# Five column sums of a hybrid trunk kernel: eight one-column products each, or four tiles of 32 columns, an ACT copy and a turn through DRAM

## The reference

```python
c_act = jax.nn.silu(c)
for i in range(DEPTH):
    mod = c_act @ ada_w[i] + ada_b[i]                       # (1, 6144)
    sh1, sc1, g1, sh2, sc2, g2 = jnp.split(mod[:, None, :], 6, axis=-1)
    h = rms_norm(x, norm_mix[i]) * (1.0 + sc1) + sh1
    y = mixer_i(h)                                          # attention or HGRN2
    x = x + g1 * y
    h = rms_norm(x, norm_ffn[i]) * (1.0 + sc2) + sh2
    x = x + g2 * swiglu(h, ffn_w1[i], ffn_w3[i], ffn_w2[i])
```

## Time and profile before

| | |
|---|---|
| time, median of 3 runs | 870.5 us (870.15 to 871.99) |
| profiled execution: its time, its span | 872.44 us, 870.6 us |
| mean granted PE clock | 0.99 |
| busy: PE, PEld, DVE | 839.7 us (96%), 699.8 us (80%), 613.9 us (71%) |
| busy: ACT, POOL | 432.6 us (50%), 137.9 us (16%) |
| DMA | 188.97 MB, mean 217 GB/s |

### The profile page before, as it was taken

The page is one execution under the profiler, slowest core; times in us unless marked ns, Lnnn a source line. Parts: engine busy times, 40 slices in busy tenths (PEclk is TensorE's granted clock), DMA queues, the critical chain, the costliest instruction groups (busy, mean ns, idle before and its releaser), DMA issues.

```text
span 870.6 us, 10955 instructions
## 1 busy us (share of the span) xinstructions
PE 839.7 (96%) x4254; PEld 699.8 (80%) x4254; DVE 613.9 (71%) x728; ACT 432.6 (50%) x549; POOL 137.9 (16%) x157
## 2 busy tenths in 40 slices
PE   4999999999999989999999989999999999999998
PEld 2778878878878878887888877888888788887886
DVE  4897798788888776577576676787867665654544
ACT  5355464464445555453344356778575744433431
POOL 3000101111010120011010020467813000000000
PEclk9799999999999999999999999999999999999999
DMA  9997878887877635688787745434234577665521
GB/s 320 365 357 238 293 253 276 283 255 234 284 260 235 229 108 193 198 275 293 260 271 255 240 145 180 156 98 146 97 117 129 208 248 234 228 206 180 192 96 49
DMA packets 122102, 188.97 MB, mean 217 GB/s; under 512 B 5683, under 2 KB 91048, under 8 KB 122052
## 3 DMA queue, kind: packets, MB, share of 16 engines
q1 hardware_dynamic: 109796, 146.10, 51.8%
q0 software_dynamic: 12256, 42.18, 14.4%
HBM read 187.18 MB, written 1.09 MB: 216 GB/s over the span
## 4 chain that ended last, share of the span: by engine, by line
PE 76%; DVE 13%; ACT 4%; issue 4%; DMA 2%; POOL 1%; SPq 0%; DVEq 0%; ACTq 0%; POOLq 0%
PE bank L526 62%; DVE wlo L1363 2%; PE bank L642 2%; DVE acc L1374 2%; DVE x L1532 2%; PE bank L722 2%; PE bank L748 1%; PE bank L916 1%; ACT whi L988 1%; PE bank L595 1%; PE bank L703 1%; PE bank L860 1%; DMA x<-in_x_dram 1%; PE bank L559 1%; DVE sq L1530 1%
## 5 line engine op out<-in xcount | busy, mean ns | idle before, releaser
L1363 DVE TENSOR_TENSOR wlo<-raw,whi 128x2048 fp32r<-128x2048 f32 x123 | 285.4, 2325 | 41.9 <-ACT whi L988 41.8
L988 ACT ACTIVATE whi<-raw 128x2048 fp32r<-128x2048 f32 (+1 forms) x124 | 235.3, 1900 | 18.9 <-DMA raw<-in_attn_w_qkv_dram 12.2
L526 PE MATMUL bank<-whi,hT_hi 128*128 128x512 f32 (+1 forms) x728 | 195.1, 391 | 2.4 <-ACT hT_hi L988 1.5
L526 PE MATMUL bank<-wlo,hT_hi 128*128 128x512 f32 (+1 forms) x752 | 194.1, 381 | 1.2 <-DVE wlo L1363 1.2
L526 PE MATMUL bank<-whi,hT_lo 128*128 128x512 f32 (+1 forms) x728 | 187.3, 380 | 0.0
L526 PEld LDWEIGHTS bank<-wlo,hT_hi 128*128 128x128 f32 x752 | 137.3, 188 | 29.5 <-DVE wlo L1363 2.0
L526 PEld LDWEIGHTS bank<-whi,hT_lo 128*128 128x128 f32 x728 | 132.9, 188 | 26.5
L526 PEld LDWEIGHTS bank<-whi,hT_hi 128*128 128x128 f32 x728 | 129.5, 188 | 29.9 <-issue 6.5
L393 POOL DMA_DIRECT2D ada_w<-in_ada_w_dram x80 | 42.7, 534 | 466.2 <-DVE acc L1374 449.0
L1374 DVE SCALAR_TENSOR_TENSOR acc<-ada_w,cact,acc 128x1024 f32<-128x1024 f32 x80 | 102.3, 1279 | 8.0 <-DMA ada_w<-in_ada_w_dram 6.0
L1224 ACT ACTIVATE arena<-bank 128x256 f32<-128x256 f32 x44 | 14.5, 381 | 166.8 <-PE bank L526 166.8
(11 more groups left out here) (184 smaller groups left out, 854.5 us busy)
## 6 DMA issues: line engine op xcount, KB each, us to landing
raw<-in_ffn_w_dram SPq DMA_DIRECT2D x88, 512.0 KB, 4.9
ada_w<-in_ada_w_dram POOLq DMA_DIRECT2D x80, 512.0 KB, 5.0
raw<-in_attn_w_qkv_dram SPq DMA_DIRECT2D x62, 512.0 KB, 6.5
raw<-in_ffn_w_dram SPq DMA_DIRECT2D x22, 1024.0 KB, 4.9
raw<-in_hgrn_w_in_dram SPq DMA_DIRECT2D x16, 1024.0 KB, 5.4
arena<-in_ada_w_dram SPq DMA_DIRECT2D x16, 512.0 KB, 10.1
raw<-in_attn_w_qkv_dram SPq DMA_DIRECT2D x4, 1024.0 KB, 7.1
raw<-in_attn_w_out_dram SPq DMA_DIRECT2D x4, 1024.0 KB, 7.4
```

Source lines behind the costliest of these rows:

```text
L526: mm = nc.tensor.matmul(dst[t][c][:, 0:n], lhs[:, k0 + k, t * P:(t + 1) * P], w[:, k, c * 512:c * 512 + n], start=start and k == 0, stop=s ...
L988: return nc.scalar.activation(dst, src, ACT.Copy)
L1363: nc.vector.tensor_tensor(wlo[:, m % RAW, :], raw[:, m % RAW, :], fp(hi_of(m)), ALU.subtract).then_inc(s["split"], 1)
```

## The change

Five of the six column tasks (`BY_ROWS`, all but task 11) take another way.

1. PE: instead of eight products with one moving column, four products with 32 columns of ones stationary and 256 columns of `acc` moving. Product i writes 32 partitions of bank 7 (32i to 32i + 31), so each has its own quarter of the array's columns. The result is a row spread over four partition groups.
2. ACT copies bank 7 (128 x 256) back into the first 256 columns of `acc` (`ada_sums`) and raises `ada_ev`; DVE did that before.
3. POOL (`turn_columns`) writes four partitions of it to a DRAM tensor `column_sums` (8 x 128), waits until that has landed, and reads it back transposed as 128 partitions x 8 single elements into `columns`.
4. DVE (`take_columns`) waits for that and takes `columns` where it took bank 7, later than before: in units 23 and 27, FFN 0 steps 6 and 16, HGRN2 step 4.
5. POOL's queue: `ada_load` of a block's first piece now comes ahead of the block's memset and bias load, not behind them, for all ten blocks. Between the two stands `turn_columns` of the block that had the same `acc`, for blocks 5, 6, 8 and 9 (which turn blocks 3, 4, 6 and 7); block 9 is turned behind the last load of the first 88.
6. DVE and ACT wait for `col_use` before they apply a modulation.

```diff
         small = sb("small", [P, 64])
+        columns = sb("columns", [P, KC])
...
+        sums = nc.dram_tensor("column_sums", (KC, P), F32, kind="Internal").ap()
...
+            def turn_columns(r):
+
+                n = BY_ROWS.index(r)
+                rows_ = acc[0:P:32, TASKS[r][0] % 2, 0:256]
+                pool.wait_ge(s["ada_ev"], r + 1)
+                if n:
+                    pool.wait_ge(s["col_use"], n)
+                pool.dma_start(sums.rearrange("(q i) p -> q (i p)", i=2), rows_).then_inc(s["col_out"], 16)
+                pool.wait_ge(s["col_out"], 16 * (n + 1))
+                pool.dma_start(columns[:], sums.rearrange("c p -> p c"), allow_slow_non_contiguous=True
+                               ).then_inc(s["col_in"], 16)
+
             def ada_load(n):
 
                 layer, b, k = n // (ADA_BLOCKS * KC), n // KC % ADA_BLOCKS, n % KC
-                if k == 0:
-
-                    blk = ADA_BLOCKS * layer + b
-                    if blk < 4:
-                        pool.wait_ge(s["mod_red"], blk - 1)
-                    else:
-                        pool.wait_ge(s["ada_red"], tasks_until(blk - 2))
-                    pool.memset(acc[:, blk % 2], 0.0).then_inc(s["ada_zero"], 1)
-                    pool.wait_ge(s["ada_zero"], blk - 1)
-                    pool.dma_start(acc[0:1, blk % 2, :], a["ada_b"][layer:layer + 1, b * ADA_COLS:(b + 1) * ADA_COLS]
-                                   ).then_inc(s[f"adab_in{blk % 2}"], 16)
                 if n == 2 * KC:
                     pool.wait_ge(s["first_sum"], 2 * KC - 1)
                 if n >= 2 * KC + ADA_RING:
                     pool.wait_ge(s["ada_used"], n - 2 * KC - ADA_RING + 1)
                 pool.dma_start(ada_w[:, n % ADA_RING], a["ada_w"][layer, k * P:(k + 1) * P, b * ADA_COLS:(b + 1) * ADA_COLS]
                                ).then_inc(ada_in[n % ADA_RING], 16)
+                if k == 0:
+
+                    blk = ADA_BLOCKS * layer + b
+                    if blk < 4:
+                        pool.wait_ge(s["mod_red"], blk - 1)
+                    else:
+                        pool.wait_ge(s["ada_red"], tasks_until(blk - 2))
+                        for r in BY_ROWS[:-1]:
+                            if TASKS[r][0] == blk - 2:
+                                turn_columns(r)
+                    pool.memset(acc[:, blk % 2], 0.0).then_inc(s["ada_zero"], 1)
+                    pool.wait_ge(s["ada_zero"], blk - 1)
+                    pool.dma_start(acc[0:1, blk % 2, :], a["ada_b"][layer:layer + 1, b * ADA_COLS:(b + 1) * ADA_COLS]
+                                   ).then_inc(s[f"adab_in{blk % 2}"], 16)
...
                 ada_load(n)
+            turn_columns(BY_ROWS[-1])
             split_second(M_IN + 1)
...
-                if kind == "row":
+                if r in BY_ROWS:
+                    for i in range(4):
+                        mm = nc.tensor.matmul(bank[7][32 * i:32 * i + 32, 0:256], ones[:, 0:32],
+                                              src[:, i * 256:(i + 1) * 256], start=True, stop=True)
+                elif kind == "row":
...
+            def ada_sums(r):
+
+                act.wait_ge(s["ada_red"], r + 1)
+                copy(acc[:, TASKS[r][0] % 2, 0:256], bank[7][:, 0:256]).then_inc(s["ada_ev"], 1)
...
             for m in range(2, PURE):
                 round_unit(m + AHEAD)
                 qkv_extra(m)
+                for r in tasks_at(m):
+                    if r in BY_ROWS:
+                        ada_sums(r)
...
+                            elif task in BY_ROWS:
+                                ada_sums(task)
...
+            def take_columns(r):
+
+                layer, what = divmod(TASKS[r][0], ADA_BLOCKS)
+                n = BY_ROWS.index(r)
+                dve.wait_ge(s["col_in"], 16 * (n + 1))
+                if what % 3 == 0:
+                    i = nc.vector.tensor_copy(mod_b[:, layer, what // 3], columns[:])
+                else:
+                    i = scale_gain(layer, what // 4, columns[:])
+                i.then_inc(s["col_use"], 1)
...
                 for r in tasks_at(m):
-                    ada_evac(r)
+                    if r not in BY_ROWS:
+                        ada_evac(r)
+                if m in (23, 27):
+                    take_columns(BY_ROWS[m // 27])
...
+                        if r in (6, 16):
+                            take_columns(BY_ROWS[2 + r // 16])
...
+                if step == 4:
+                    take_columns(BY_ROWS[4])
...
+BY_ROWS = [r for r, (_, kind, _) in enumerate(TASKS) if kind != "row" and r != HGRN_TASK]
```

More of the change, by code:

```diff
@@ L209, in hybrid_trunk @@
             first_sum first_mm mod_red mod_sum mod_ev
-            ada_used ada_red ada_ev adab_in0 adab_in1 ada_zero h0_raw h0_aff
+            ada_used ada_red ada_ev col_out col_in col_use adab_in0 adab_in1 ada_zero h0_raw h0_aff
             tab_mm tab_cp
@@ L373, in _ @@
             pool.dma_start(tabw, a["distance_table"]).then_inc(s["rel_in"], 16)
+            def turn_columns(r):
[8 more added lines that the diff above has]
+                               ).then_inc(s["col_in"], 16)
             def ada_load(n):
                 layer, b, k = n // (ADA_BLOCKS * KC), n // KC % ADA_BLOCKS, n % KC
+                if n == 2 * KC:
+                    pool.wait_ge(s["first_sum"], 2 * KC - 1)
+                if n >= 2 * KC + ADA_RING:
+                    pool.wait_ge(s["ada_used"], n - 2 * KC - ADA_RING + 1)
+                pool.dma_start(ada_w[:, n % ADA_RING], a["ada_w"][layer, k * P:(k + 1) * P, b * ADA_COLS:(b + 1) * ADA_COLS]
+                               ).then_inc(ada_in[n % ADA_RING], 16)
                 if k == 0:
@@ L388, in ada_load @@
                                    ).then_inc(s[f"adab_in{blk % 2}"], 16)
[L389 to L394, removed]
             def split_second(m):
@@ L1042, in norm_round @@
                 act.wait_ge(s["xn_tr"], 4 * q + 2 * t + 2)
+                act.wait_ge(s["col_use"], (2, 4, 5)[q - 1])
                 for kc in range(4, KC):
@@ L1487, in norm_affine @@
                 dve.wait_ge(s["xn_tr"], 4 * q + 2 * t + 1)
+                dve.wait_ge(s["col_use"], (2, 4, 5)[q - 1])
                 for kc in range(4):
@@ L1691, in ffn @@
                         for task in tasks_at(M_FFN0 + r):
-                            if TASKS[task][0] != 5:
+                            if TASKS[task][0] != 5 and task not in BY_ROWS:
                                 ada_evac(task)
+                        if r in (6, 16):
+                            take_columns(BY_ROWS[2 + r // 16])
             ffn(0, M_FFN0)
```

## The result

The changed kernel took 874.27 us (median of 5 runs, 873.43 to 874.88) against 870.5 (5 runs): ratio 1.0039, 95% interval 1.0027 to 1.0050. It is slower by 3.8 us, as forecast in sign, but the forecast was 10.1. The profiled execution took 874.88 us, span 872.1.

The account below looks back on a forecast made before the run. Around the changed sums PE and DVE were taken to hand the chain to each other. Terms -1.5 + 5.2 + 4.0 + 3.4 + 0.3 - 1.3 = +10.1 us on a median of 870.5 gave 880.6 us, range 869.5 to 888.

Parts of the forecast that it names:

- PE's tiles: Five column tasks on PE: 1.38 us each against 1.68, 0.3 saved a task, -1.5 us in all.
- stall, block 5: DVE's op of block 5 starts 7.0 us late for its bias; less 1.77 slack, PE loses +5.2 us.
- stall, block 6: DVE's op of block 6 starts 7.7 us late; after slack on DVE and PE, PE loses +4.0 us.
- clock behind both: PE's granted clock halves after the stalls at blocks 5 and 6, 1.7 us lost each, +3.4 us.
- other blocks: Blocks 4 and 7 under 1 us late, +0.3 us in all; blocks 8 and 9 nothing.
- given back: DVE catches up while PE is held or slow, so PE's 1.28 us wait at 212 goes: -1.3 us.
- I take the middle: Pricing PE's tiled tasks from line 911: overlap by 1.7, 1.08 us plus 0.30, between bounds +1.7 and -4.8 us in all.
- POOL's queue: Turn, memset and bias load now stand behind a block's first load, so DVE's ops of blocks 5 and 6 start late.
- W: Turn's write of four rows to DRAM, issue to landing: taken as 4.9 us, bounds 3.4 and 6.0.
- G: Issue of the turn's element-wise read back from DRAM: taken as 1.0 us, bounds 0.5 and 4.4.
- B: Bias load on POOL's queue, issue to landing: 4.9 us (3.4 to 6.0).
- Rival (b): DVE's wait is covered and only PE's term is left: 869.0 us, or 865.7 with tiles side by side; chance 0.13.

Follow-up runs that it names:

- e5: e1 with all four products of a sum on the same 32 array columns and the same 32 partitions of bank 7: 871.54 us, ratio 1.0007 to the kernel before.
- e6: e1 with the eight one-column products of before in place of the four tiled ones, ACT's copy and turn kept: 871.88 us, ratio 1.0005 to the kernel before.
- e4: The changed kernel with four dummy float32 products on PE ahead of the attention's transposes behind units 23 and 28: 871.48 us, ratio 1.0003 to the kernel before.
- e1: The changed kernel with turn, memset and bias load of a block again ahead of its first piece's load: 864.29 us, ratio 0.9923 to the kernel before.
- e2: The kernel before with only POOL's order changed, each block's first load ahead of its memset and bias load: 867.39 us, ratio 0.9961.
- e9: The kernel before with memset and bias load behind the first piece's load for blocks 6 and 7 only: 868.84 us, ratio 0.9977.
- e8: The changed kernel with only the turn ahead of a block's first load, memset and bias load behind it: 864.50 us, ratio 0.9922 to the kernel before.
- e10: e9 with one extra memset at each of the two old places, ahead of the first piece's load: 870.66 us, ratio 0.9994 to the kernel before.
- e3: The changed kernel without the two transfers of each turn, POOL setting the columns to zero instead: 863.15 us, ratio 0.9906 to the kernel before.

## Why the prediction was wrong

The forecast's own terms, with what the paired profiles measured. The measured ones add up to 3.1 us, the last row of the table of starts to 3.2:

| term | forecast | measured |
|---|---|---|
| PE's tiles | -1.5 | -5.1 |
| stall, block 5 | +5.2 | +3.4 |
| stall, block 6 | +4.0 | +3.7 |
| clock behind both | +3.4 | +4.9 |
| other blocks | +0.3 | +0.5 (block 7) |
| given back | -1.3 | -2.3 (memsets) |
| clock at the norms | none | -2.0 |

Outside the span, and so in none of these rows, lies another +0.5 us that the forecast had at nothing.

- **PE's tiles: mis-sized, the largest error.** The step that failed is "I take the middle because line 911 is the same kind of tile". Line 911 uses two tiles in turn, not four, so a factor of 2 is the most that its row can show, and 1.7 is close to it: in the trace its records start in pairs 7 ns apart, with 32 ns from pair to pair, where 27 are needed for 32 columns. The row did not speak for "the second record of a product waits and neighbours overlap by one"; it spoke for tiles side by side. In the changed kernel four tiles ran wholly side by side: a task costs 0.57 + 0.10 + 0.03 = 0.70 us (records to next matmul; entry, 161.84 less 161.09 + 0.82 - 0.27 + 0.11; slower first matmuls) instead of 1.71. Five tasks make -5.1, a little beyond the lower bound of the forecast, -4.8. e5 and e6 confirm mechanism and size.
- **POOL's queue: right.** W and G came within 1 us, B within 1.3, and the whole way from the load's issue to the bias' landing took 11.7 and 12.2 us instead of 12.6. At block 5 the weight matmul ahead of the wait came 2.85 us earlier than before (185.88 against 188.73). Counted from there, DVE's op was 6.1 us late (forecast 7.0), its normalisation, with the slack of 1.77 used up as forecast, 4.3 (192.06 and 193.47), and PE's transposes of 194.60 (now 196.02) 4.3 as well. Of these 4.3, 3.4 are idle time (3.56 + 0.33 - 0.51); 0.7 lie in the transposes of line 753, which already ran at half clock (1.54 instead of 0.82 us) and count in the next row.
- **The clock behind the stalls: right in kind** (e4), low by 1.5 us, as the first stall brought 6.8 us at half clock and not 3.4. The 4.9 are what is left of 5.3 and 5.6 us when idle time and the task are taken out.
- **Other blocks: right.** DVE waited 1.1 us for block 7's bias (priced at under 1), and that cost 0.5.
- **Given back: right in size by half, wrong in reason.** The wait of 1.28 us at 212 did go, but not because DVE caught up: it goes as well in e1, e2 and e9, which have no stall there. It was the memset that held DVE's small op, and there were two.
- **The norms: not in the sum.** I took it as certain that 2.3 us of idle PE lowers the clock. In the 12 profiles PE waited 2.30 to 2.33 us at norm 1 and 2.42 to 2.46 at norm 2, and the clock fell in 6 and in 5 of them. The changed kernel's profile had neither, that of before both. In the paired starts full clock at norm 1 is worth 1.6 us to every version that had it, e2 included, and nothing to e8, which had not; at norm 2 it is worth 0.75, and nothing to e2. This moves single executions by up to 2.4 us; it isn't the change's doing. Between medians it can't be told how much of 3.8 us it is.
- The time lay in the range (869.5 to 888) and the sign held, but 10.1 us were forecast and 3.8 measured. The errors don't cancel: all but those of the clock behind the stalls, of block 7 and of what lies outside the span made the changed kernel faster than forecast. The sign held because the two stalls with their clock (12.0) outweigh the tiles and the memsets (7.4). Rival (b), that only PE's term is left, is what e1 made of the change: 864.3.
- Rule and trace: the Trainium skill ("TensorEngine Tiling (Array Packing)", Key Properties) says that tiles work independently. I weighed that sentence less than line 911's row; e5's 1.91 us on one tile against 0.64 on four agrees with it. The Trainium skill ("DMA: Bandwidth & Descriptors", Anatomy of one DMA) has 2.0 us for a small DMA; here the writes took 4.0 and 5.9, and the trace decides.

## What to carry to other kernels

A step that waits on a queue is to be put ahead of the issue that must leave late anyway, not behind it: the same turn cost 10 us behind one load and nothing ahead of it. Where a row of a similar shape serves as a price, count the tiles that it uses: a row on two tiles can't show what four do. Column sums were cheap on four column tiles with 256 moving columns (0.70 us instead of 1.71); shorter ones were not tried. Before pricing a move on POOL, look in the trace for small DVE ops that last as long as a POOL op beside them: here two moved memsets gave 2.3 us that nobody had priced.

## What the runs showed of the hardware

- **A memset of POOL holds a DVE op.** Eight columns of `TENSOR_SCALAR`, 0.17 us alone, took 1.37 to 1.38 us when a memset of 128 x 1024 ran, and ended with it; put the memset back (e10) and it returns. In the 12 profiles this op met such a memset 7 times and was long each time, and with it the small op right behind it (1.30 us, line 1449). Other ops that met a memset were as long as ever: subtractions of two SBUF operands into `wlo` (2.28 us, 58 times), and `TENSOR_SCALAR` of one column (0.15 to 0.21 us, 5 times). Those of 384 columns were a little longer, 0.51 to 0.60 us instead of 0.42. The Trainium skill ("SBUF — State Buffer", Who interferes with whom) says that DVE and GpSimd share a pair of ports, that `tensor_scalar` can take it and `tensor_tensor` with both inputs in SBUF meets only GpSimd's reads, and that the second to come waits in full; the long op and the subtractions agree. DVE's record starts 0.37 us before the memset's, so who came first can't be read from it, and that the ports are the cause is argued, not shown.
- **Other work of POOL does the same.** The last of DVE's takes, of the same 8 columns, took 1.49 us instead of 0.17 in all eight versions that have it, and in the changed kernel it ended at 561.40 us, as a `TENSOR_TENSOR` of POOL did (557.80 to 561.38). The forecast had the takes at nothing, and that held: the paired starts of the changed kernel show no step there.

```profile
L1461 DVE COPY mod_b<-columns x3: 164/167/1485, 200.4 to 559.9; 128x8 f32<-128x8 f32 x3
```

- **Half clock behind idle PE.** Waits of 2.3 to 2.5 us were followed by it in 11 of 24 cases, the stalls of 2.9 to 3.7 us each time (four, in two profiles of the changed kernel). Of the shorter waits behind 50 us, the 12 of 1.3 to 1.7 us never were; the single one of 1.9 us (e3, at 66 us) was.
- **One-column products can be followed by half clock without idle.** In e2 the stretch behind the task after unit 23 ran at 0.50, with a wait of only 0.51 us ahead of it; the same in e9, and in e1 and e4 behind the one-column task of block 10. Two more, in e1 and e2 at 46 us, lie behind the one-column products of the start, with a wait of 0.3 us ahead. But of the 37 such tasks behind 150 us in the 12 profiles only four were followed by it, and e6 and e10 have six each and none. Behind a tiled task without a stall (28) it was not seen. So this is an observation and no rule. The timeline of e2 at that task, and its windows ahead of and behind it (columns as above):

```profile
194.34 1.84 PE L595 MATMUL bank<-ones,acc 128*128 128x1 f32 x16
```
```profile
190.00:196.00 6.00, 5.49 (x38) 4.75 (x36) 5.86 (x11) 5.33 (x8) 1.08 (x2) 1.00 0.79 232
196.60:199.80 3.20, 3.20 (x9) 2.45 (x8) 3.20 (x4) 0.94 (x3) 0.53 (x1) 0.50 0.94 296
```
